# Attention of a two-layer diffusion step: the softmax division moved from the probabilities to the outputs

## The chip, the cores and the metric

The kernel runs on one core of a Trainium2 chip. The metric is the device time of one execution in microseconds (us), the median of three runs. One execution was also recorded by the hardware profiler, instruction by instruction; that record is the trace, and its summary is the profile's page.

## The reference, cut to what matters

One step of a hybrid backbone with two layers. Each layer is a half-step SwiGLU feed-forward block, a token mixer, and another half-step feed-forward block; the mixer of layer 0 is attention, that of layer 1 a spatial gating unit. Only the attention is touched here. It has 128 context tokens and 256 latent tokens, 16 heads of 64 numbers: 8 of neighbourhood attention (NA, with a bias on the latent scores) and 8 of grouped-query attention (GQA, no bias, 2 key heads).

```python
s = einsum(q * D ** -0.5, k)             # per head: 128 x 128 (context), 256 x 384 (latent)
p = softmax(s, axis=-1)                  # exp(s - max) / sum
o = einsum(p, v)                         # 64 numbers per query
```

Context queries see the 128 context keys of the step. Latent queries see 256 latent keys and 128 cached keys in one softmax. The outputs of all heads are concatenated and multiplied by `w_out`.

## The kernel before, in words

The program is written out by engine, each engine with its own list of instructions in a fixed order and waits on semaphores between them. Weights come in 1 MB panels (`raw`), which ScalarE rounds to a high part (`w_hi`, 1.9 us) and VectorE completes with a low part (`w_lo`); every weight product is three TensorE passes over high and low parts. The activations that feed a weight product are split in the same way, into `x_hi` and `x_lo`.

The attention stage stands between the panels of the q/k/v projection and those of the output projection (`Q_OUT0`, four panels). Heads go in eight pairs, in the order `TURNS = (0, 4, 1, 5, 2, 6, 3, 7)`: pairs under 4 are NA, the others GQA, so NA and GQA alternate, and turn n is the n-th pair. A turn has three steps, `s = 3n, 3n+1, 3n+2`: the context queries (below called C, 128 keys) and the two blocks of 128 latent queries (L1 and L2, 384 keys). All 128 queries of a step lie on the partitions, and both heads of the pair are handled together. A step goes through these stations:

- `scores(s)`, TensorE: two products into banks 5 and 6, or 0 and 1 in alternate steps. It waits for the exponentials of step s-2, which free the banks.
- `top(s)`, VectorE: for latent NA steps the bias is added, then the negated row maximum is taken (`nmax`).
- `softmax(s)`, ScalarE: exponential into `prob`, with the row sum in `rsum`.
- `normalise(s)`, VectorE: reciprocal of the sum, and a product over the whole of `prob` (128 x 768 numbers in a latent step).
- `p_transposes(s)`, TensorE: two or six transposes of 128 x 128 into banks 3 and 4, which are used in every step, so that they wait for the copy of step s-1.
- `put_pT(s)`, ScalarE: the copy of the transposed probabilities out of the banks (`pT_ctx`, `pT_lat`).
- `values(n)`, TensorE, once per turn: the products with v, transposed outputs (head numbers on the partitions, tokens along the row) into bank 7 or 2. It stands in step 3n+3, behind the transposes of that step.
- `o_hi(n)` on ScalarE and `o_lo(n)` on VectorE split the output straight from the bank into `x_hi` and `x_lo`.

TensorE runs two steps ahead: in step i it does `scores(i+2)`, then `p_transposes(i)`, and in every third step `values`. In steps 0 to 2 TensorE and ScalarE also finish the last transposes of q (`TR_LATE`, copied by `put_group`, semaphore `tr_act`). The last turn is folded into the first panel of the output projection (`last_pair`): TensorE does two output banks, the last transposes, two more banks, `values(7)`, and the other four banks. The split of the second output panel (`split(Q_OUT0 + 1)`) stands on ScalarE behind `o_hi(7)` and on VectorE behind `o_lo(7)`.

## Time and profile before

| what | value |
|---|---|
| median of 3 runs | 1561.32 us (1557.76 to 1566.09) |
| profiled execution, its time | 1559.92 us |
| its span in the trace | 1558.1 us |
| TensorE busy | 1519.7 us, 98% of the span |
| VectorE busy | 1073.2 us, 69% |
| ScalarE busy | 616.3 us, 40% |
| mean granted clock of TensorE | 0.995 of full speed |
| attention stage, first scores to the second output panel | 412.4 to 479.9 us |

The span is what the instructions cover; 1.8 us of the execution's time lie around it. TensorE's busy share is that of matmuls that overlap each other's fill and drain, so a high share doesn't say that the engine never waits. The attention stage is about 67 us, or 4% of the span.

### The profile page before, as it was taken

The numbers are of one execution on the slowest core, as the hardware profiler recorded it, in microseconds if no ns is written. First come the engines' busy times: TensorE is split into PE (matmuls) and PEld (weight loads), VectorE is DVE, ScalarE is ACT, GpSimd is POOL, SyncE is SP. The second block draws the span as 40 slices with busy tenths as digits, with TensorE's granted clock in tenths as the row PEclk, the third lists the DMA queues.
The fourth block names the chain that finished last, engine by engine and source line by source line (L and its number), as shares of the span: only waits on it lengthen the run. The fifth ranks groups of instructions, "written<-read, shape, count | busy, mean of one in ns | idle before, by whom it ended". The sixth has DMA issues, their size and how long they took to land.

```text
span 1558.1 us, 23355 instructions
## 1 busy us (share of the span) xinstructions
PE 1519.7 (98%) x9159; PEld 1491.8 (96%) x9159; DVE 1073.2 (69%) x1423; ACT 616.3 (40%) x840; POOL 74.0 (5%) x59
## 2 busy tenths in 40 slices
PE   6999999989899999999999999999999999999999
PEld 6899999989759999999999999999999999999999
DVE  6886777868897866768877667797767567443323
ACT  3452332164583643322355233226643246333221
POOL 2000000023100100000020000002000010000000
PEclk9999999989999999999999999999999999999999
DMA  9345465736403244465624545563552533333332
GB/s 386 112 141 211 166 228 205 261 139 230 139 1 140 104 172 178 180 250 193 241 86 154 220 162 216 216 252 130 195 206 82 216 109 108 135 111 133 135 112 91
DMA packets 49937, 262.68 MB, mean 169 GB/s; under 512 B 6608, under 2 KB 7888, under 8 KB 27984
## 3 DMA queue, kind: packets, MB, share of 16 engines
q1 hardware_dynamic: 49872, 261.79, 45.9%
q8 instruction: 44, 0.72, 0.2%
q14 instruction: 21, 0.17, 0.0%
HBM read 259.54 MB, written 2.23 MB: 168 GB/s over the span
## 4 chain that ended last, share of the span: by engine, by line
PE 84%; DVE 6%; issue 4%; DMA 2%; ACT 2%; SPq 1%; POOL 0%; DVEq 0%; ACTq 0%
PE ps L1288 24%; PE ps L1290 24%; PE ps L1289 24%; PE ps L1322 3%; PE ps L1325 3%; PE ps L1323 3%; DVE mprod L827 2%; ACT w_hi L537 1%; DMA raw<-panels 1%; DMA raw_x<-panels 1%; DVE x_lo L890 1%; DVE w_lo L819 1%; DVE h L1011 1%; PE ps L1612 1%; PE ps L1516 1%
## 5 line engine op out<-in xcount | busy, mean ns | idle before, releaser
L819 DVE TENSOR_TENSOR w_lo<-raw,w_hi 128x2048 fp32r<-128x2048 f32 x163 | 373.2, 2289 | 305.0 <-ACT w_hi L537 303.6
L537 ACT ACTIVATE w_hi<-raw 128x2048 fp32r<-128x2048 f32 x164 | 314.2, 1916 | 666.7 <-PE ps L1290 506.4
L1288 PE MATMUL ps<-x_hi,w_hi 128*128 128x384 f32 (+1 forms) x1520 | 515.9, 339 | 9.8 <-DVE x_lo L890 8.6
L1289 PE MATMUL ps<-x_lo,w_hi 128*128 128x384 f32 (+1 forms) x1520 | 513.1, 338 | 0.0
L1290 PE MATMUL ps<-x_hi,w_lo 128*128 128x384 f32 (+1 forms) x1520 | 512.7, 337 | 0.0
L827 DVE SCALAR_TENSOR_TENSOR mprod<-mraw,cB 128x1024 f32<-128x1024 f32 x256 | 313.2, 1224 | 7.8
L1288 PEld LDWEIGHTS ps<-x_hi,w_hi 128*128 128x128 f32 x1520 | 286.6, 189 | 13.2 <-issue 7.4
L1289 PEld LDWEIGHTS ps<-x_lo,w_hi 128*128 128x128 f32 x1520 | 286.9, 189 | 0.7
L1290 PEld LDWEIGHTS ps<-x_hi,w_lo 128*128 128x128 f32 x1520 | 286.6, 189 | 0.0
L1290 PE MATMUL ps<-act_hi,w_lo 128*128 (+1 forms) x832 | 279.6, 336 | 0.0
L1288 PE MATMUL ps<-act_hi,w_hi 128*128 (+1 forms) x832 | 279.6, 336 | 0.0
L1289 PE MATMUL ps<-act_lo,w_hi 128*128 (+1 forms) x832 | 279.6, 336 | 0.0
L1288 PEld LDWEIGHTS ps<-act_hi,w_hi 128*128 128x128 f32 x832 | 156.4, 188 | 0.0
L1289 PEld LDWEIGHTS ps<-act_lo,w_hi 128*128 128x128 f32 x832 | 156.4, 188 | 0.0
L1290 PEld LDWEIGHTS ps<-act_hi,w_lo 128*128 128x128 f32 x832 | 156.4, 188 | 0.0
L1322 PE MATMUL ps<-w_hi,x_hi 128*128 128x256 f32 x408 | 116.0, 284 | 3.0 <-ACT x_hi L564 2.4
L1323 PE MATMUL ps<-w_lo,x_hi 128*128 128x256 f32 x408 | 115.4, 283 | 0.0
L1325 PE MATMUL ps<-w_hi,x_lo 128*128 128x256 f32 x408 | 114.3, 283 | 0.0
L1322 PEld LDWEIGHTS ps<-w_hi,x_hi 128*128 128x128 f32 x408 | 77.7, 191 | 4.5 <-issue 4.5
L1323 PEld LDWEIGHTS ps<-w_lo,x_hi 128*128 128x128 f32 x408 | 77.8, 191 | 0.0
L1325 PEld LDWEIGHTS ps<-w_hi,x_lo 128*128 128x128 f32 x408 | 77.2, 191 | 0.0
L504 POOL TENSOR_TENSOR sqsum<-sq 128x384 f32<-128x384 f32 x6 | 9.7, 1621 | 1004.1 <-ACT sq L578 731.1
(154 smaller groups left out, 1148.4 us busy)
## 6 DMA issues: line engine op xcount, KB each, us to landing
raw<-panels SPq DMA_DIRECT2D x164, 1024.0 KB, 5.2
mraw<-mod_rows SPq DMA_DIRECT2D x128, 512.0 KB, 3.5
raw_x<-panels SPq DMA_DIRECT2D x5, 1024.0 KB, 6.0
mshift<-mod_rows SPq DMA_DIRECT2D x8, 512.0 KB, 15.5
mscale<-mod_scale SPq DMA_DIRECT2D x6, 512.0 KB, 12.2
bias<-na_bias SPq DMA_DIRECT2D x4, 512.0 KB, 6.4
h<-x_in_t SPq DMA_DIRECT2D x1, 1536.0 KB, 11.0
out<-h SPq DMA_DIRECT2D x4, 384.0 KB, 2.3
```

Source lines behind the costliest of these rows:

```text
L537: nc.scalar.activation(w_hi[q0 % 2][:, :], raw[q0 % 2][:, :], ACT.Copy).then_inc(hi_done, 1)
L819: nc.vector.tensor_tensor(w_lo[q0 % 2][:, :], raw[q0 % 2][:, :], w_hi[q0 % 2][:, :].bitcast(F32), ALU.subtract).then_inc(lo_done, 1)
L827: nc.vector.scalar_tensor_tensor(product[:, :], rows, 1.0, cB[:, cond, :], ALU.mult, ALU.mult, accum_out=out[:, cond:cond + 1]).then_inc(m ...
L890: last = nc.vector.scalar_tensor_tensor(x_lo[:, m, cols], h[:, m, cols], aT[:, m, cond:cond + 1], x_hi[:, m, cols].bitcast(F32), ALU.mult, ...
L1011: last = nc.vector.scalar_tensor_tensor(h[:, m, cols], ps[:, m, cols], gT[:, m, cond:cond + 1], h[:, m, cols], ALU.mult, ALU.add)
L1288: mm(out, w[0][:, cols], xs[0], start=start, stop=False)
L1289: mm(out, w[0][:, cols], xs[1], start=False, stop=False)
L1290: return mm(out, w[1][:, cols], xs[0], start=False, stop=stop)
L1322: mm(out, x_hi[:, k, tok], hi[:, cols], start=(k == 0), stop=False)
L1323: mm(out, x_hi[:, k, tok], lo[:, cols], start=False, stop=False)
L1325: last = mm(out, x_lo[:, k, tok], hi[:, cols], start=False, stop=(k == KD - 1))
L1516: last = nc.tensor.transpose(ps[:, 3 + a, P * k:P * k + P], prob[:, s % 3, a, P * k:P * k + P], ident[:, :])
```

## The change

The probabilities are no longer divided. The exponentials are transposed and multiplied with v as they are, and the outputs are divided by the sums. Since outputs lie with the tokens along the row, the reciprocals are needed along the row too. Per turn, `divisor` takes the six reciprocals of the turn (three steps, two heads) in one VectorE instruction, repeats each 64 times with a copy into `tmp[:, 2]` (128 x 384), TensorE transposes that in three pieces into bank 2 (`divisor_rows`), ScalarE copies the bank to `tmp[:, 1]` (`put_divisor`), and VectorE multiplies bank 7 with it into `tmp[:, 0]` (`o_divided`), from where `o_hi` and `o_lo` read. Bank 2 is no longer a second bank for the outputs. The copies out of the transposed probabilities' banks are shared: VectorE takes those of C steps in all turns, and of L1 steps in GQA turns; ScalarE keeps the rest.

```diff
--- before.py
+++ after.py
@@ -139,8 +139,8 @@
         hms = sb("hms", [P, 12])
         hrs = sb("hrs", [P, 12])
         nmax = sb("nmax", [P, 3, 2])
-        rsum = sb("rsum", [P, 3, 2])
-        rinv = sb("rinv", [P, 3, 2])
+        rsum = sb("rsum", [P, 2, 3, 2])
+        rinv = sb("rinv", [P, 4, 2])
         vss = sb("vss", [P, TT, KD])
 
 
...
@@ -340,6 +343,9 @@
         def span(s):
 
             return NCTX if s % 3 == 0 else T
+
+        def copied_by_vector(s):
+            return s % 3 == 0 or (s % 3 == 1 and TURNS[s // 3] >= 4)
 
         def scored(s):
 
...
@@ -699,41 +705,48 @@
                 act.wait_ge(nmax_done, s + 1)
                 if s >= 3:
                     act.wait_ge(pT_pe, s - 2)
+                if s >= 6 and s % 3 == 0:
+                    act.wait_ge(rinv_done, s // 3 - 1)
                 for a in range(2):
                     last = nc.scalar.activation(prob[:, s % 3, a, 0:span(s)], scored(s)[:, a, :], ACT.Exp,
-                                                bias=nmax[:, s % 3, a:a + 1], accum_out=rsum[:, s % 3, a:a + 1])
+                                                bias=nmax[:, s % 3, a:a + 1], accum_out=rsum[:, s // 3 % 2, s % 3, a:a + 1])
                 last.then_inc(exp_done, 1)
 
             def put_pT(s):
                 pair, kind = divmod(s, 3)
                 act.wait_ge(pT_pe, s + 1)
-                if kind == 0:
-                    if pair >= 2:
-                        act.wait_ge(o_pe, pair - 1)
-                    nc.scalar.activation(pT_ctx[:, pair % 2, :, :], ps[:, 3:5, 0:P], ACT.Copy).then_inc(pT_done, 1)
-                else:
-                    if pair:
-                        act.wait_ge(o_pe, pair)
-                    nc.scalar.activation(pT_lat[:, :, :, P * (kind - 1):P * kind],
-                                         ps[:, 3:5, 0:T].rearrange("p a (k q) -> p a k q", k=3), ACT.Copy) \
-                        .then_inc(pT_done, 1)
+                if pair:
+                    act.wait_ge(o_pe, pair)
+                nc.scalar.activation(pT_lat[:, :, :, P * (kind - 1):P * kind],
+                                     ps[:, 3:5, 0:T].rearrange("p a (k q) -> p a k q", k=3), ACT.Copy) \
+                    .then_inc(pT_done, 1)
+
+            def put_divisor(turn):
+                act.wait_ge(div_pe, turn + 1)
+                if turn:
+                    act.wait_ge(o_scaled, turn)
+                nc.scalar.activation(tmp[:, 1, 0:T], ps[:, DIV_BANK, 0:T], ACT.Copy).then_inc(div_done, 1)
 
             def o_hi(turn):
-                act.wait_ge(o_pe, turn + 1)
-                nc.scalar.activation(x_hi[:, TURNS[turn], 0:T], ps[:, O_BANK[turn % 2], 0:T], ACT.Copy).then_inc(oh_done, 1)
+                act.wait_ge(o_scaled, turn + 1)
+                nc.scalar.activation(x_hi[:, TURNS[turn], 0:T], tmp[:, 0, 0:T], ACT.Copy).then_inc(oh_done, 1)
 
             softmax(0)
             put_group(8)
             put_group(9)
             softmax(1)
             for i in range(STEPS):
-                put_pT(i)
+                if not copied_by_vector(i):
+                    put_pT(i)
+                if i and i % 3 == 0:
+                    put_divisor(i // 3 - 1)
                 if i + 2 < STEPS:
                     softmax(i + 2)
                 for j in TR_LATE.get(i, ()):
                     put_group(j)
-                if i and i % 3 == 0:
+                if i > 3 and i % 3 == 1:
                     o_hi(i // 3 - 1)
+            put_divisor(7)
             o_hi(7)
             split(Q_OUT0 + 1, 0)
             down(Q_OUT0, KD // 2, lambda: split_spare(1))
...
@@ -1169,30 +1182,55 @@
                     link(nc.vector.tensor_tensor(v, v, bias[:, kind - 1, 2 * pair:2 * pair + 2, :], ALU.add))
                 nc.vector.tensor_reduce(nmax[:, s % 3, :], scored(s), AX.X, ALU.max, negate=True).then_inc(nmax_done, 1)
 
-            def normalise(s):
-                dve.wait_ge(exp_done, s + 1)
-                link(nc.vector.reciprocal(rinv[:, s % 3, :], rsum[:, s % 3, :]))
-                v = prob[:, s % 3, :, 0:span(s)]
-                nc.vector.tensor_tensor(v, v, rinv[:, s % 3, :, None].to_broadcast([P, 2, span(s)]), ALU.mult) \
-                    .then_inc(prob_done, 1)
+            def put_pT(s):
+                pair, kind = divmod(s, 3)
+                dve.wait_ge(pT_pe, s + 1)
+                if kind == 0:
+                    if pair >= 2:
+                        dve.wait_ge(o_pe, pair - 1)
+                    nc.vector.tensor_copy(pT_ctx[:, pair % 2, :, :], ps[:, 3:5, 0:P]).then_inc(pT_done, 1)
+                else:
+                    dve.wait_ge(o_pe, pair)
+                    nc.vector.tensor_copy(pT_lat[:, :, :, P * (kind - 1):P * kind],
+                                          ps[:, 3:5, 0:T].rearrange("p a (k q) -> p a k q", k=3)).then_inc(pT_done, 1)
+
+            def divisor(turn):
+                dve.wait_ge(exp_done, 3 * turn + 3)
+                if turn:
+                    dve.wait_ge(div_pe, turn)
+                link(nc.vector.reciprocal(rinv[:, 0:TT, :], rsum[:, turn % 2, :, :]))
+                nc.vector.tensor_copy(tmp[:, 2, 0:T].rearrange("p (t a d) -> p t a d", a=2, d=HD),
+                                      rinv[:, 0:TT, :, None].to_broadcast([P, TT, 2, HD])).then_inc(rinv_done, 1)
+
+            def o_divided(turn):
+                dve.wait_ge(o_pe, turn + 1)
+                if turn:
+                    dve.wait_ge(ol_done, turn)
+                dve.wait_ge(div_done, turn + 1)
+                nc.vector.tensor_tensor(tmp[:, 0, 0:T], ps[:, O_BANK, 0:T], tmp[:, 1, 0:T], ALU.mult) \
+                    .then_inc(o_scaled, 1)
 
             def o_lo(turn):
-                pair = TURNS[turn]
+                dve.wait_ge(o_scaled, turn + 1)
                 dve.wait_ge(oh_done, turn + 1)
-                nc.vector.tensor_tensor(x_lo[:, pair, 0:T], ps[:, O_BANK[turn % 2], 0:T], x_hi[:, pair, 0:T].bitcast(F32),
+                nc.vector.tensor_tensor(x_lo[:, TURNS[turn], 0:T], tmp[:, 0, 0:T], x_hi[:, TURNS[turn], 0:T].bitcast(F32),
                                         ALU.subtract).then_inc(ol_done, 1)
 
             dve.wait_ge(bias_in, 64)
             top(0)
             top(1)
-            normalise(0)
             for i in range(STEPS):
                 if i + 2 < STEPS:
                     top(i + 2)
-                if i + 1 < STEPS:
-                    normalise(i + 1)
-                if i > 3 and i % 3 == 1:
-                    o_lo(i // 3 - 1)
+                if copied_by_vector(i):
+                    put_pT(i)
+                if i and i % 3 == 0:
+                    o_divided(i // 3 - 1)
+                if i % 3 == 2:
+                    divisor(i // 3)
+                    if i > 3:
+                        o_lo(i // 3 - 1)
+            o_divided(7)
             o_lo(7)
             split(Q_OUT0 + 1, 0)
             down(Q_OUT0, KD // 2, 1, (0, 1), 1.0, MOD_M + MOD_IN, MOD_OUT, spare=1)
...
@@ -1508,7 +1546,7 @@
                 last.then_inc(s_pe, 1)
 
             def p_transposes(s):
-                pe.wait_ge(prob_done, s + 1)
+                pe.wait_ge(exp_done, s + 1)
                 if s:
                     pe.wait_ge(pT_done, s)
                 for a in range(2):
...
@@ -1516,12 +1554,20 @@
                         last = nc.tensor.transpose(ps[:, 3 + a, P * k:P * k + P], prob[:, s % 3, a, P * k:P * k + P], ident[:, :])
                 last.then_inc(pT_pe, 1)
 
+            def divisor_rows(turn):
+                pe.wait_ge(rinv_done, turn + 1)
+                if turn:
+                    pe.wait_ge(div_done, turn)
+                for t in range(TT):
+                    last = nc.tensor.transpose(ps[:, DIV_BANK, P * t:P * t + P], tmp[:, 2, P * t:P * t + P], ident[:, :])
+                last.then_inc(div_pe, 1)
+
             def values(turn):
 
                 pair = TURNS[turn]
+                if turn:
+                    pe.wait_ge(o_scaled, turn)
                 pe.wait_ge(pT_done, 3 * turn + 3)
-                if turn >= 2:
-                    pe.wait_ge(ol_done, turn - 1)
                 v, cache = (v_na, vc_na) if pair < 4 else (vg_, vc_g)
                 for keys, out_cols, start, stop in ((-1, slice(0, P), True, True), (0, slice(P, T), True, False),
                                                     (1, slice(P, T), False, False), (2, slice(P, T), False, True)):
...
@@ -1529,7 +1575,7 @@
                         cols = slice(HD * (2 * pair + a), HD * (2 * pair + a) + HD) if pair < 4 else slice(HD * a, HD * a + HD)
                         w = cache[:, cols] if keys == 2 else v[:, keys + 1, cols]
                         moving = pT_ctx[:, turn % 2, a, :] if keys < 0 else pT_lat[:, a, keys, :]
-                        last = mm(ps[HD * a:HD * a + HD, O_BANK[turn % 2], out_cols], w, moving, start=start, stop=stop)
+                        last = mm(ps[HD * a:HD * a + HD, O_BANK, out_cols], w, moving, start=start, stop=stop)
                 last.then_inc(o_pe, 1)
 
             pe.wait_ge(tr_act, 5)
...
@@ -1548,24 +1594,27 @@
                     pe.wait_ge(tr_act, 10)
                 if i + 2 < STEPS:
                     scores(i + 2)
+                if i == 3:
+                    pe.wait_ge(tr_act, 13)
+                if i and i % 3 == 0:
+                    divisor_rows(i // 3 - 1)
                 p_transposes(i)
                 for j in TR_LATE.get(i, ()):
                     pe.wait_ge(tr_act, j - 1)
                     transposed(j)
-                if i == 3:
-                    pe.wait_ge(tr_act, 13)
                 if i and i % 3 == 0:
                     values(i // 3 - 1)
 
             def ready_attn(m):
                 if m == 5:
                     pe.wait_ge(exp_done, STEPS - 1)
+                    pe.wait_ge(ol_done, 6)
                 elif m == 0:
                     pe.wait_ge(exp_done, STEPS)
                 elif m == 4:
                     pe.wait_ge(pT_done, STEPS)
                 elif m == 7:
-                    pe.wait_ge(ol_done, 7)
+                    pe.wait_ge(o_scaled, 8)
                 elif m == 2:
                     pe.wait_ge(ol_done, 8)
 
...
@@ -1574,6 +1623,7 @@
                 some((5, 6))
                 p_transposes(STEPS - 1)
                 some((0, 1))
+                divisor_rows(NH - 1)
                 values(NH - 1)
                 return some((4, 3, 7, 2))
 
```

What stands in each engine's list is read from the two programs. First VectorE, from the maximum of turn 2's C step (an NA turn) to the work behind the maximum of its L2 step; `nmax<-ps` are the maxima, `ps<-ps,bias` the bias. Before:

```order
L1170 TENSOR_REDUCE nmax<-ps 128x2
L1174 RECIPROCAL rinv<-rsum 128x2
L1176 TENSOR_TENSOR prob<-prob,rinv 128x768
L1182 TENSOR_TENSOR x_lo<-ps,x_hi 128x384
L1169 TENSOR_TENSOR ps<-ps,bias 128x2x256
L1170 TENSOR_REDUCE nmax<-ps 128x2
L1174 RECIPROCAL rinv<-rsum 128x2
L1176 TENSOR_TENSOR prob<-prob,rinv 128x2x128
L1169 TENSOR_TENSOR ps<-ps,bias 128x2x256
L1170 TENSOR_REDUCE nmax<-ps 128x2
L1174 RECIPROCAL rinv<-rsum 128x2
L1176 TENSOR_TENSOR prob<-prob,rinv 128x768
```

And of the change, for the same stretch:

```order
L1183 TENSOR_REDUCE nmax<-ps 128x2
L1194 COPY pT_lat<-ps 128x6x128
L1182 TENSOR_TENSOR ps<-ps,bias 128x2x256
L1183 TENSOR_REDUCE nmax<-ps 128x2
L1201 RECIPROCAL rinv<-rsum 128x6
L1202 COPY tmp<-rinv 128x384
L1216 TENSOR_TENSOR x_lo<-tmp,x_hi 128x384
L1182 TENSOR_TENSOR ps<-ps,bias 128x2x256
L1183 TENSOR_REDUCE nmax<-ps 128x2
L1191 COPY pT_ctx<-ps 128x256
L1210 TENSOR_TENSOR tmp<-ps,tmp 128x384
```

The three products over `prob` (turn 1's L2 step, turn 2's C and L1) and the three small reciprocals are gone. In their place are the copy of turn 1's L1 step (`pT_lat<-ps`), the reciprocal and the repeat of turn 1 (`rinv<-rsum` of six, `tmp<-rinv`) behind turn 2's L1 maximum, the copy of turn 2's C step, and the product with the divisors.

Next TensorE, at the end of turn 1: the scores of its L2 step (GQA), the transposes of turn 1's C step, and the values of turn 0. Before:

```order
L1507 MATMUL ps<-kT_g,qT_g 128x384 x2
L1516 MATMUL ps<-ident,prob 128x128 x2
L1532 MATMUL ps<-pT_ctx,v_na 64x128 x2
L1532 MATMUL ps<-pT_lat,v_na 64x256 x4
L1532 MATMUL ps<-pT_lat,vc_na 64x256 x2
```

And of the change:

```order
L1545 MATMUL ps<-kT_g,qT_g 128x384 x2
L1562 MATMUL ps<-ident,tmp 128x128 x3
L1554 MATMUL ps<-ident,prob 128x128 x2
L1578 MATMUL ps<-pT_ctx,v_na 64x128 x2
L1578 MATMUL ps<-pT_lat,v_na 64x256 x4
L1578 MATMUL ps<-pT_lat,vc_na 64x256 x2
```

Three transposes of `tmp` (the repeated reciprocals of turn 0) stand between the scores and the transposes of the probabilities, seven times in the loop; an eighth group stands in front of the last `values`.

Last ScalarE, at the end of the stage. Before:

```order
L703 ACTIVATE prob,rsum<-ps,nmax 128x384 x2
L723 ACTIVATE x_hi<-ps 128x384
L717 ACTIVATE pT_lat<-ps 128x6x128 x2
L723 ACTIVATE x_hi<-ps 128x384
L537 ACTIVATE w_hi<-raw 128x2048 x3
```

And of the change:

```order
L711 ACTIVATE prob,rsum<-ps,nmax 128x384 x2
L732 ACTIVATE x_hi<-tmp 128x384
L720 ACTIVATE pT_lat<-ps 128x6x128
L728 ACTIVATE tmp<-ps 128x384
L732 ACTIVATE x_hi<-tmp 128x384
L543 ACTIVATE w_hi<-raw 128x2048 x3
```

The last high part (`x_hi`) is now read from `tmp` and so stands behind VectorE's product, which is not in this list; the copy of the divisors (`tmp<-ps`) is new, one per turn.

## Rows read from the trace of the kernel before

Rows of the timeline give the start in us, the duration, the engine, line, operation, output and inputs; in brackets the idle time before it and what ended it.

**Rows 1.** The page: span, and busy time of each engine.

```profile
span 1558.1 us, 23355 instructions
PE 1519.7 (98%) x9159; PEld 1491.8 (96%) x9159; DVE 1073.2 (69%) x1423; ACT 616.3 (40%) x840; POOL 74.0 (5%) x59
```

**Rows 2.** Windows, from one pair's last scores group to the next pair's.

```profile
core 0: us, PE busy (x) PEld busy (x) DVE busy (x) ACT busy (x) POOL busy (x), PEclk, DMA share, GB/s
424.57:431.45 6.88, 5.87 (x44) 3.37 (x43) 4.81 (x9) 5.50 (x17) 0.00 (x0) 1.00 0.01 2
451.42:457.55 6.13, 5.84 (x43) 3.37 (x42) 5.16 (x11) 5.22 (x16) 0.00 (x0) 1.00 0.00 0
457.55:464.48 6.93, 5.94 (x43) 3.37 (x43) 6.76 (x13) 5.44 (x16) 0.00 (x0) 1.00 0.00 0
```

**Rows 3.** Windows of 2 us where the granted clock changes.

```profile
418.00:420.00 2.00, 0.61 (x5) 0.45 (x6) 1.97 (x4) 1.38 (x6) 0.00 (x0) 1.00 1.00 371
420.00:422.00 2.00, 2.00 (x11) 1.67 (x13) 1.19 (x3) 1.23 (x4) 0.00 (x0) 0.56 0.96 262
```

**Rows 4.** Timeline, TensorE: one group of turn 1, then turns 5 and 6.

```profile
421.71 1.65 PE L1507 MATMUL ps<-kT_g,qT_g 64*128 64x384 f32 x4
...
451.42 0.92 PE L1507 MATMUL ps<-kT_g,qT_g 64*128 64x384 f32 x4
...
452.48 0.41 PE L1516 MATMUL ps<-ident,prob 128*128 128x128 f32 x2
...
454.49 0.49 PE L1507 MATMUL ps<-kT_na,qT_na 64*128 64x128 f32 x4
...
454.91 0.88 PE L1516 MATMUL ps<-ident,prob 128*128 128x128 f32 x6
...
455.71 0.92 PE L1507 MATMUL ps<-kT_na,qT_na 64*128 64x384 f32 x4
...
456.75 0.64 PEld L1516 LDWEIGHTS ps<-ident,prob 128*128 128x128 f32 x6 [0.73 <-DVE prob L1176]
...
457.55 0.92 PE L1507 MATMUL ps<-kT_na,qT_na 64*128 64x384 f32 x4
...
459.17 0.44 PE L1516 MATMUL ps<-ident,prob 128*128 128x128 f32 x2 [0.70 <-DVE prob L1176]
```

**Rows 5.** Timeline, VectorE and ScalarE, in the same stretch.

```profile
452.39 0.96 DVE L1170 TENSOR_REDUCE nmax<-ps 128x2 f32<-128x768 f32 x1 [0.35 <-PE ps L1507]
...
455.82 0.81 ACT L717 ACTIVATE pT_lat<-ps 128x768 f32<-128x768 f32 x1 [0.58 <-PE ps L1516]
...
458.50 0.15 DVE L1174 RECIPROCAL rinv<-rsum 128x2 f32<-128x2 f32 x1
...
459.03 0.69 DVE L1169 TENSOR_TENSOR ps<-ps,bias 128x512 f32<-128x512 f32 x1
...
460.75 0.58 ACT L703 ACTIVATE prob<-ps,nmax 128x384 f32<-128x384 f32 x1 [0.63 <-DVE nmax L1170]
```

**Rows 6.** Groups by line and form, whole kernel, VectorE.

```profile
L1176 DVE TENSOR_TENSOR prob<-prob,rinv 128x768 f32<-128x768 f32 x16 | 15.3, 958 | 0.6
L1182 DVE TENSOR_TENSOR x_lo<-ps,x_hi 128x384 fp32r<-128x384 f32 x8 | 4.4, 552 | 6.2 <-ACT x_hi L723 6.2
L884 DVE COPY sqsum<-ps 128x384 f32<-128x384 f32 x5 | 2.8, 557 | 15.3 <-PE ps L1375 15.3
L1248 DVE TENSOR_SCALAR wsn<-wsT,rs 128x1024 f32<-128x1024 f32 x3 | 2.1, 750 | 1.0 <-POOL rs L522 1.0
```

**Rows 7.** Timeline: the first values group (turn 0) and the end of the stage.

```profile
426.72 0.44 PE L1532 MATMUL ps<-pT_ctx,v_na 128*64 128x128 f32 x4 [0.86 <-ACT qT_g L668]
...
473.47 0.44 PE L1532 MATMUL ps<-pT_ctx,vg_ 128*64 128x128 f32 x4
...
475.25 0.49 ACT L723 ACTIVATE x_hi<-ps 128x384 fp32r<-128x384 f32 x1 [2.98 <-PE ps L1532]
...
479.92 0.45 PE L1288 MATMUL ps<-x_hi,w_hi 128*128 128x384 f32 x1 [0.27 <-DVE w_lo L819]
```

More of the change, by code:

```diff
@@ L262, in build @@
         exp_done = sem("exp_done")
-        prob_done = sem("prob_done")
+        rinv_done = sem("rinv_done")
+        o_scaled = sem("o_scaled")
+        div_pe = sem("div_pe")
+        div_done = sem("div_done")
         pT_pe = sem("pT_pe")
@@ L692, in _ @@
                 if g == 7:
-                    nc.scalar.activation(rsum[:, 2, 0:1], mhalf[:, 0:1], ACT.Exp)
+                    nc.scalar.activation(rsum[:, 0, 2, 0:1], mhalf[:, 0:1], ACT.Exp)
                 for i in TR_AFTER[g]:
@@ L1652 @@
 S_BANK = (5, 0)
-O_BANK = (7, 2)
+O_BANK, DIV_BANK = 7, 2
 TR_AFTER = ((), (), (), (), (0, 1), (2, 3), (4, 5), (6, 7), ())
@@ L1663, in tr_bank @@
 def tr_bank(i):
-    return 3 + i % 2 if i < 8 else O_BANK[i % 2]
+    return 3 + i % 2 if i < 8 else (O_BANK, DIV_BANK)[i % 2]
 _OUTS = [(P, KD, T), (1, 1, NCTX, NH, HD), (1, 1, NCTX, NH, HD), (1, 1, NCTX, 2, HD), (1, 1, NCTX, 2, HD)]
```

## The prediction

> **What bounds the kernel now.** I read the page first: 1519.7 us of TensorE in a span of 1558.1 [rows 1], so outside the attention any gain on another engine is covered by weight products. Then the windows, cut at TensorE's last scores group of each turn (S2; S0, S1 and S2 are a turn's three scores groups, T0, T1, T2 its transposes, V the values, D the new transposes of the reciprocals). An interval from a GQA turn's S2 to an NA turn's takes 6.13 us, one from NA to GQA 6.93 [rows 2]. In the longer VectorE is busy for 6.76 of 6.93 us; in the shorter for 5.16 of 6.13. TensorE's 5.84 and 5.94 us look nearly full too, but pipelined matmuls overstate it, so I read the timeline for spacings [rows 4]. S0 takes 0.42 until the next group can start (454.49 to 454.91) though it is busy for 0.49; a 384-column group, busy for 0.92, then takes 0.85. Six transposes take 0.80 (454.91 to 455.71). T0 and V together take 2.01 (452.48 to 454.49). One interval therefore needs of TensorE S2 0.85, T0 and V 2.01, S0 0.42, T1 0.80, S1 0.85, T2 0.80: 5.73 us. The rest is waiting: 0.21 in front of T0 and 0.19 in front of T2 when the next turn is NA (5.73 + 0.40 = 6.13), and 1.2 when VectorE has the bias in front of it, where the chain of waits runs through VectorE and T0 starts at 459.17 instead of 458.40 [rows 4]. So VectorE's queue bounds half of the intervals, and TensorE is only 0.4 us from bounding the others.
>
> **The change, part by part.**
>
> VectorE loses, per turn, two products of 0.96 [rows 6], one of 256 numbers, 0.42 (on the line through 0.552 for 384 and 0.958 for 768), and three reciprocals; it gains a reciprocal of 0.15 [rows 5], the repeat, a division of 128 x 384 from PSUM, which I price as the existing subtraction of that form, 0.55 [rows 6], a C copy of 256 numbers, 0.42 by the same line, and in GQA turns a copy of 128 x 768 out of PSUM. That copy has no row; a copy of 384 takes 0.557 against 0.552 for a two-operand instruction of that width, so 768 will take what the product of 768 takes, 0.96 [rows 6]. For the repeat, SBUF to SBUF with 384 numbers out, the bounds are 0.28 (750 ns for 1024 numbers of a one-operand instruction, in proportion) and 0.557 (a copy of the same width from PSUM) [rows 6]. I take 0.557: same operation, same width. Balance: 2.8 us off and about 1.7 (NA) or 2.6 (GQA) on. VectorE stops being full.
>
> The Trainium skill ("VectorE: DVE Perf Modes", Mode 2×_2P) says that an fp32 copy runs at two numbers a cycle if source and destination lie in SBUF, and not out of PSUM. The first half would give the repeat about 0.28 and the sum 0.8 less; the second agrees with the row of 0.557 for a PSUM copy.
>
> TensorE gains D, three transposes: half of six, 0.40, eight times, 3.2 us, all on the engine that is nearly full. The interval's own work becomes 6.13. That is the floor: the average now is 6.53, so the most that the loop can win is 0.4 per turn.
>
> Waits that stay or come. (a) T0 waited for the product; it now needs only the exponential and stands behind D, so 0.21 goes. (b) T2 waits for the copy of T1 out of the same banks: T1 to T2 is 1.84 where work takes 1.65, hence 0.19. It stays in NA turns. In GQA turns the copy is VectorE's, 0.96 instead of 0.81 [rows 5], so 0.34. (c) D waits for the reciprocals, and those stand on VectorE behind the next turn's L1 maximum. Count from S2 of a GQA turn at 0, next turn NA: D to 1.25, T0 and V to 3.26, S0 to 3.68, T1 to 4.48, S1 from 4.48, T2 from 5.67 (b), next S2 at 6.47, D could start at 7.32. VectorE: scores reach it 0.97 after their start (451.42 to 452.39 [rows 4, 5]), so 5.45; its copy of T1 ends at 5.5; bias and maximum run until 1.72 later (459.03 to 460.75 [rows 5]), less 0.1 that the next instruction overlaps, so 7.1; reciprocal with its self-wait 0.2; repeat 0.56; signal 0.12: 7.97. D waits 0.65 and with it T0, V and all behind. With the next turn GQA the maximum has no bias: the repeat ends about 0.75 earlier, no wait. Behind the repeat VectorE still has `o_lo`, then the L2 bias and maximum; those end at 9.9 or 3.4 after S2, and their exponential is wanted by S1 at about 5.1: covered by V. ScalarE gains a copy of 384 (0.49, as its existing one [rows 7]) and loses the C copy in all turns and one of 0.81 in GQA turns; it stays below 5.5 us an interval and is covered.
>
> So an interval from GQA to NA takes 6.13 + 0.34 = 6.47 (now 6.13), one from NA to GQA 6.13 + 0.19 + 0.65 = 6.97 (now 6.93). From turn 2's S2 to turn 7's there are three of the longer and two of the shorter: 33.85 against 33.05, **+0.8 us**. The interval before, now 6.88 [rows 2], is different: V of turn 0 waits until 426.72 for ScalarE's last copy of q [rows 7]. That wait moves ahead of D. ScalarE has one copy less before it and the exponentials come a product earlier; counting its list the copy ends about 1.3 us sooner, of which D and T0 take 0.4 and 0.35 back: **-0.4 us**, with bounds of -1.4 (all kept) and +0.2.
>
> End of the stage. From turn 7's S2 to T2 of the loop, D adds 0.40 and the 0.4 of waits for products go: 0. Then D stands ahead of the last V, 0.40. After it, V starts at 473.47, ScalarE's high part at 475.25, then the split of the second panel, for which TensorE waits until 479.92 [rows 7]. The wait is already there, so everything put into that chain counts: the division 0.55 and a handover of 0.03. Together **+1.0 us**. If TensorE had had other work it would cost nothing; it has none.
>
> Sum: 0.8 - 0.4 + 0 + 1.0 = +1.4 us on 1559.92, the profiled execution's own time: 1561.3. The shown median is 1.4 us above that execution, so I name 1561.5 and let the range take the spread.
>
> **The rivals.**
>
> (1) *Forecast: given back.* VectorE's relief turns into D on TensorE and the wait (c), with a longer end: 1561.3. Chance 0.60.
>
> (2) *The relief is kept.* Waits (b) and (c) vanish if VectorE runs its list sooner than I count (repeat at 0.28, small instructions overlapping). All intervals at 6.13: 30.65, -2.4; start down to -1.4; end +1.0: 1557.1. For it: (c) is a difference of two sums over eight instructions. Against: (b) is two row spacings. Chance 0.26.
>
> (3) *VectorE's queue delays D in every turn,* as it would if the copies out of PSUM are dearer than 0.96: every interval 6.13 + 0.34 + 0.65 = 7.12, five give 35.6, +2.55; start +0.2, end +1.0: 1563.7. It decides, meaning over 0.5%, only when an interval reaches 7.6 us or more, 1.1 above the present mean in each of some seven. Chance 0.08.
>
> (4) *Slower: TensorE's clock falls for the stage.* The granted clock fell to 0.56 in 420 to 422, right after two microseconds in which TensorE was busy for 0.61 of 2.00 [rows 3]: between its levels, 1.2 and 2.4 GHz. A scores group then took 1.65 instead of 0.92 [rows 4], 1.8 times. An interval at the lower level would be 6.13 x 1.8 = 11.0, 4.5 more, over some seven and a half: +34 us, 1594. Against it: in all intervals of rows 2 the clock stayed at 1.00, with 1.94 of each 5.73 us in transposes, and the change leaves TensorE fewer gaps. It decides if the engine's work per interval thins out as in the window from 418. Chance 0.04.
>
> On this the Trainium skill ("TensorE: Matmul & The Clock Gate", Part 4: PE-mode transpose) says that a transpose does not count as activity for the full clock as a matmul does. That speaks against more transposes; the trace shows full clock throughout a stage with 14 transposes per turn, and 17 will hardly differ.
>
> (5) *A gain over 0.5%.* It would need 7.8 us of a stage whose floor allows 2.4 in the loop. Chance 0.02.
>
> **Numbers.** 0.5% (7.8 us) is about what a measurement of this kernel can tell from no change. Cases 1 to 3 lie within 4 us of the time before; with the spread of single runs (3.6 below and 4.8 above the median) they give "same" 0.92, slower 0.05, faster 0.03. The range takes 1557.1 and 1563.7 and, for the median's own wandering, another 1 to 3 us: 1556 to 1567.
>
> **What the profile would show.** Right: VectorE clearly below 6.76 us in NA-to-GQA intervals; these intervals at about 7.0, with TensorE idle in front of L1562 until the repeat (L1202), and about 6.5 the other way; the second output panel 7.0 us behind the start of the last V (now 6.45). Wrong: D never waits (then case 2), the repeat at half its price, T0 waiting for VectorE's copies, or a clock under 1.00 behind 424. Most likely to be wrong is (c): a shift of 0.3 us in VectorE's list changes three intervals by as much.

## Result, and the profile after

The changed kernel takes 1570.9 us (median of 10 runs, 1566.2 to 1572.76), the one before 1562.28 (10 runs, 1557.76 to 1566.72). The ratio is 1.0053 [1.0043, 1.0064]: 8.6 us slower, outside the range of 1556 to 1567. The profiled execution took 1570.92 us.

The page of the changed kernel, span and engines, against [rows 1]:

```profile
span 1569.1 us, 23425 instructions
PE 1531.6 (98%) x9183; PEld 1505.1 (96%) x9183; DVE 1067.1 (68%) x1411; ACT 614.4 (39%) x836; POOL 74.1 (5%) x59
```

VectorE is busy for 6.1 us less. TensorE is busy for 11.9 us more, and has only 24 matmuls more. Eight groups of three small transposes, 3.2 us of work, can't be 11.9. So I cut the execution into three pieces at starts of `w_lo` panels (VectorE's low parts, numbered from 0 to 162): up to panel 40, in front of the attention; 40 to 43, the attention stage; 43 to 162, all that follows.

| us | to panel 40 | 40 to 43 | 43 to 162 |
|---|---|---|---|
| before | 412.41 | 78.27 | 1049.34 |
| changed | 417.71 | 77.41 | 1055.79 |

The stage that the diff rewrites is 0.86 us shorter. The loss lies outside it, 6.45 us behind it and 5.3 ahead of it. (The piece ahead wanders, 412.4 to 417.7 over the 13 profiles of this study. Part of it doesn't: from the first to the last product of 384 columns, the first feed-forward block takes 224.58 us before and 228.68 in the changed kernel, 4.1 more. What wanders is the stretch between this block and the attention, 92.4 to 96.2 us, with no order by layout. What follows therefore rests on the last piece and on medians.)

Where behind it? The start of a low part at the head and at the end of ten panels of the second feed-forward block, VectorE's timeline of the kernel before:

```profile
636.20 2.29 DVE L819 TENSOR_TENSOR w_lo<-raw,w_hi 128x2048 fp32r<-128x2048 f32 x1 [3.98 <-ACT w_hi L537]
...
719.40 2.29 DVE L819 TENSOR_TENSOR w_lo<-raw,w_hi 128x2048 fp32r<-128x2048 f32 x1 [0.73 <-ACT w_hi L537]
```

and of the changed kernel:

```profile
641.20 2.29 DVE L832 TENSOR_TENSOR w_lo<-raw,w_hi 128x2048 fp32r<-128x2048 f32 x1 [5.21 <-ACT w_hi L543]
...
725.04 2.29 DVE L832 TENSOR_TENSOR w_lo<-raw,w_hi 128x2048 fp32r<-128x2048 f32 x1 [0.80 <-ACT w_hi L543]
```

Ten panels take 83.20 us before and 83.84 now. VectorE isn't the cause: it sits idle ahead of these instructions for longer than before. A panel is 48 TensorE products with 384 columns, so they follow each other every 173.3 ns before and every 174.7 ns now. A window of 100 us in the last feed-forward block shows the same thing without VectorE. Kernel before, then changed (columns as in [rows 2]):

```profile
1400.00:1500.00 100.00, 100.00 (x579) 100.00 (x578) 35.84 (x22) 28.73 (x20) 0.00 (x0) 1.00 0.36 126
```

```profile
1400.00:1500.00 100.00, 100.00 (x575) 100.00 (x574) 36.58 (x22) 29.55 (x22) 0.00 (x0) 1.00 0.36 126
```

TensorE is never idle in either, the granted clock is 1.00 in both, the DMA moves the same bytes, and it gets through 575 matmuls instead of 579. The spacing is uniform (between 1400 and 1460 us no two starts lie further apart than 0.18 us), with no gap at a panel's head. So no wait was added: every such product is 0.8% slower, in code that the diff doesn't touch.

In two stretches of the changed kernel the loss per product is larger: in the first feed-forward block and in the gating unit's output projection the products follow each other every 176.5 to 176.7 ns, where the kernel before has 173.3 to 173.5. A window of 60 us in that projection, kernel before and then changed:

```profile
1211.00:1271.00 60.00, 60.00 (x348) 60.00 (x347) 31.09 (x34) 18.34 (x13) 0.00 (x0) 1.00 0.48 176
```

```profile
1215.00:1275.00 60.00, 60.00 (x342) 60.00 (x341) 30.12 (x30) 16.65 (x10) 0.00 (x0) 1.00 0.49 177
```

The stretches account for the last piece: three feed-forward blocks of 1,296 such products take 1.72 us more each (224.47 to 226.19), and the projection's 384 products 1.28 more (66.39 to 67.67), together 6.44 of the 6.45 us.

What the diff does reach is where buffers lie. Buffers are placed one behind the other in slots of 32 bytes per partition. `rsum` grew from 24 to 48 bytes, one slot to two (`rinv`'s 24 to 32 still fit in one). So `x_hi`, `x_lo`, `x2_hi`, `x2_lo`, `act_hi`, `act_lo` and all else behind `rsum` moved by 32 bytes. The weights (`raw`, `w_hi`, `w_lo`), which lie ahead of it, did not. The addresses below follow from the programs' lists of buffers; no trace shows them.

| byte address per partition | `w_hi` | `x_hi` | `act_hi` |
|---|---|---|---|
| before | 45184 (0 mod 64) | 112032 (32 mod 64) | 161312 (32 mod 64) |
| changed | 45184 (0) | 112064 (0) | 161344 (0) |

`x2_hi` and `x2_lo` hold the activations of the later gate and up panels (the views print them as `x_hi` and `x_lo`, without the number); they stand at the same place modulo 64 as `x_hi` in every kernel here. Their tiles and those of `act_hi` lie a multiple of 64 bytes apart. The tiles of `x_hi` itself are 386 numbers long and lie 1544 bytes apart, so each stands 8 bytes further on modulo 64, and the 386-column products that read them hardly differ: 178.8 ns before, 179.0 in the changed kernel. The theory below is therefore about the 384-column products with `x2` and `act`.

**The stage itself.** The windows of two intervals, against [rows 2]:

```profile
435.29:441.94 6.65, 6.19 (x46) 3.69 (x46) 5.27 (x10) 5.28 (x16) 0.00 (x0) 1.00 0.01 2
441.94:448.36 6.42, 6.12 (x46) 3.69 (x45) 4.95 (x11) 4.77 (x16) 0.00 (x0) 1.00 0.00 1
```

From GQA to NA an interval takes 6.42 (was 6.13), from NA to GQA 6.65 (was 6.93). Turn 2's S2 to turn 7's is 32.78 us (was 33.03). The timeline around D, TensorE and VectorE, against [rows 4, 5]:

```profile
434.52 0.85 PE L1554 MATMUL ps<-ident,prob 128*128 128x128 f32 x6 [0.30 <-DVE pT_lat L1194]
435.29 0.92 PE L1545 MATMUL ps<-kT_na,qT_na 64*128 64x384 f32 x4
435.89 0.18 DVE L1201 RECIPROCAL rinv<-rsum 128x6 f32<-128x6 f32 x1
436.10 0.36 DVE L1202 COPY tmp<-rinv 128x384 f32<-128x384 f32 x1
436.52 0.55 PE L1562 MATMUL ps<-ident,tmp 128*128 128x128 f32 x3 [0.31 <-DVE tmp L1202]
```

Both forecast waits are here. T2 waits for VectorE's copy, and D starts at 436.52 where the spacing of a scores group (0.85) would have let it start at 436.14: 0.38 us. The end of the stage, VectorE, ScalarE and TensorE, against [rows 7]:

```profile
477.27 0.44 PE L1578 MATMUL ps<-pT_ctx,vg_ 128*64 128x128 f32 x4
479.05 0.56 DVE L1210 TENSOR_TENSOR tmp<-ps,tmp 128x384 f32<-128x384 f32 x1 [4.94 <-PE ps L1578]
479.64 0.53 ACT L732 ACTIVATE x_hi<-tmp 128x384 fp32r<-128x384 f32 x1 [1.77 <-DVE tmp L1210]
482.01 2.29 DVE L832 TENSOR_TENSOR w_lo<-raw,w_hi 128x2048 fp32r<-128x2048 f32 x1 [1.18 <-ACT w_hi L543]
484.36 0.44 PE L1326 MATMUL ps<-x_hi,w_hi 128*128 128x384 f32 x1 [0.97 <-DVE w_lo L832]
```

The second output panel starts 7.09 us behind the last V (forecast 7.0).

### The profile page after: what moved, and what is told of

It is laid out like the page before. It is cut to its first block, busy times and chain, and to the rows that moved or that the text cites. A ratio compares the mean times of both kernels' runs of the same rounds, so it can differ in the third digit from the quotient of the medians.

```text
span 1569.1 us, 23425 instructions
## 1 busy us (share of the span) xinstructions
PE 1531.6 (98%) x9183; PEld 1505.1 (96%) x9183; DVE 1067.1 (68%) x1411; ACT 614.4 (39%) x836; POOL 74.1 (5%) x59
## 4 chain that ended last, share of the span: by engine, by line
PE 86%; DVE 5%; issue 3%; DMA 3%; ACT 2%; SPq 1%; POOL 0%; DVEq 0%; ACTq 0%
PE ps L1326 25%; PE ps L1328 25%; PE ps L1327 25%; PE ps L1360 3%; PE ps L1361 3%; PE ps L1363 3%; DVE mprod L840 2%; DMA raw<-panels 1%; ACT w_hi L543 1%; DMA raw_x<-panels 1%; PE ps L1578 1%; DVE x_lo L903 1%; DVE w_lo L832 1%; DVE h L1024 1%; PE ps L1662 1%
```

## The experiments

The theory: where the buffers lie sets the pace of TensorE's 384-column products, and that is the whole loss (A); in the form that e5 and e6 test, it is how the two operands' addresses stand to each other modulo 64 bytes (R). Its rivals: the longer instruction lists of the changed program (B); the stage's new work and what it sets off later (C); or the place of one operand decides, whatever the other does (M for the moving operand, the activations; W for the weights). "Before" in the ratios is the kernel before, run on the same chip.

**e1: only the address.** The kernel before, with a slot added ahead of `x_hi`:

```diff
         vss = sb("vss", [P, TT, KD])
+        sb("pad", [P, 8])
```

> The kernel before with nothing changed but 32 bytes per partition allocated ahead of x_hi, so that x_hi, x_lo, x2, act_hi, act_lo and all that is allocated behind them stand 32 bytes higher, as they do in the changed kernel (its rsum and rinv are larger). No instruction is added. Theory A (place in memory: the 384-column products over these buffers are paced at 174.7 ns instead of 173.3, in the first FFN 176.7): 9 to 12 us slower than before, 1571 to 1574, with panels of 8.385 us in the last FFN instead of 8.318. Theory B (code: the longer instruction lists of the changed kernel put loops and instruction fetch elsewhere): no change, 1562. Theory C (the attention stage with its new waits): no change, 1562.

**e2: only the rest.** The changed kernel, with `rinv` placed behind `act_lo`, which gives the slot back:

```diff
-        rinv = sb("rinv", [P, 4, 2])
...
         act_lo = sb("act_lo", [P, KF, T], F32R)
+        rinv = sb("rinv", [P, 4, 2])
```

> The changed kernel with rinv allocated behind act_lo, so that x_hi and everything behind it stand at the addresses of before; same instructions as the changed kernel. Theory A: the attention stage's own effect is left, which the two traces put at -0.9 us up to the output projection: 1560 to 1563, panels of 8.318 us. Theory B: as the changed kernel, 1571. Theory C: 1571.

**e3: a slot of 64 bytes.** As e1, with `[P, 16]`.

> The kernel before with 64 bytes ahead of x_hi instead of 32. Theory A1 (what counts is the address modulo 64): as before, 1562. Theory A2 (a larger modulus, or any shift costs): slower, 1566 to 1574. Theories B and C: 1562.

Measured: e1 1569.37 us, ratio 1.0048 [1.0035, 1.0061]; e2 1562.38, 1.0003 [0.9991, 1.0016]; e3 1559.81, 0.9995 [0.9982, 1.0007]. An unused slot in the old kernel brings nearly the whole loss, and the new attention at the old addresses, with all its longer lists, brings none. e1 stayed under the 1571 to 1574 that were expected: in its profile the first feed-forward block ran at 174.7 ns, not at the changed kernel's 176.6. From panel 43 on e1 takes 1055.86 us (the changed kernel 1055.79), e2 1049.39 and e3 1049.21 (before 1049.34). So neither the new work nor the code is the cause. The move counts modulo 64: by 64 bytes nothing happens.

**e4: only the activations of the down projections.** The slot stands behind `region_d`, so `act_hi` and `act_lo` move and `x_hi` stays.

```diff
         sb("region_d", [P, KS, T])
+        sb("pad", [P, 8])
```

> The kernel before with 32 bytes between region_d and the buffers that share the memory of act_hi and act_lo: only the FFN activations (moving operand of the down panels), the attention buffers and the gating unit's move, x_hi, x_lo and x2 stay. Theory A: only the down panels slow down, 832 x 3 products of 384 columns by 1.4 ns each = +3.5 us (to +8 if it is 3.4 ns as in the first FFN), 1565 to 1570, gate and up panels unchanged at 8.32. Theories B and C: 1562.

Measured 1563.49, ratio 1.0012 [1.0002, 1.0021]: the range was missed, the direction not. By TensorE's own starts in the last three blocks: the products with `x2_hi` and `x2_lo`, which stayed, follow each other every 173.3 ns, as before; those with `act_hi` and `act_lo`, which moved, every 174.7 (before 173.3). So the pace follows each buffer by itself. Of the 3.5 us that were expected (832 x 3 = 2,496 products at 1.4 ns) the profile has 2.5 from panel 43 on and 0.7 in the first block. The medians have 2.3, and the interval reaches from 0.3 to 3.3.

**e5: everything moves together.** A slot ahead of `h`, so weights and activations both stand 32 bytes further on.

```diff
+        sb("pad", [P, 8])
         h = sb("h", [P, KD, T])
```

> The kernel before with 32 bytes ahead of h, its first buffer: the weights' buffers w_hi and w_lo move to 32 modulo 64 (from 0) and x_hi, x_lo, x2, act_hi and act_lo to 0 modulo 64 (from 32). Theory M (the address of the moving operand alone counts, 32 modulo 64 is the faster): as the 32-byte pad before, gate and up panels of the second FFN at 8.384 us and a median of 1569. Theory R (it counts that weights and moving operand stand at different places modulo 64): panels of 8.320 us and 1561.

**e6: the weights move to where the activations are.** As e5, with `rinv` behind `act_lo`, so that `x_hi` keeps 112032 and `w_hi` goes to 45216: both 32 mod 64.

> The kernel before with 32 bytes ahead of h and rinv allocated behind act_lo, so that only the buffers from h to rsum move by 32 bytes, the weights' buffers among them (now 32 modulo 64), and x_hi, x_lo, x2, act_hi, act_lo stay where they are (32 modulo 64). Theory M: panels of 8.320 us, 1561. Theory R: weights and moving operand now stand at the same place modulo 64, so 8.384 us and 1569. Theory W (the weights' own address counts): slower or faster here and in the run with everything moved alike.

Measured: e5 1562.45, ratio 1.0000 [0.9989, 1.0012]; e6 1575.9, 1.0088 [1.0073, 1.0103]. e5 has the activations at 0 mod 64, as the slow kernels have, and is as fast as before; e6 has them at the fast kernels' own address and is the slowest of all. So the activations' place alone doesn't decide. Nor does the weights': they stand at 32 in both. Only the relation is left. (Nor can it be e6's other move, `rinv` to the end: e2 has it and is fast.) Here is the window of 1400 to 1500 us of e5, then of e6:

```profile
1400.00:1500.00 100.00, 100.00 (x579) 100.00 (x578) 35.17 (x21) 28.73 (x20) 0.00 (x0) 1.00 0.36 126
```

```profile
1400.00:1500.00 100.00, 100.00 (x571) 100.00 (x570) 36.26 (x22) 29.05 (x22) 0.00 (x0) 1.00 0.35 126
```

579 as before, and 571. The theory has e6's sign and not its size: I had expected about 1569. The ten panels of e6, first and last start in VectorE's timeline:

```profile
631.05 2.29 DVE L820 TENSOR_TENSOR w_lo<-raw,w_hi 128x2048 fp32r<-128x2048 f32 x1
...
715.32 2.29 DVE L820 TENSOR_TENSOR w_lo<-raw,w_hi 128x2048 fp32r<-128x2048 f32 x1 [0.77 <-ACT w_hi L538]
```

84.27 us for 480 products, 175.6 ns each. (The first gap falls one panel ahead of the rows shown above for the other kernels, in the same block.)

**e11: the changed kernel with the weights moved instead.** e2 plus e5's slot: `w_hi` at 32, `x_hi` at 0 mod 64, as the changed kernel has it.

> The changed kernel with rinv behind act_lo and 32 bytes ahead of h: weights' buffers at 32 modulo 64, x_hi, x_lo, x2, act_hi, act_lo at 0 modulo 64, as these last are in the changed kernel as it was given. Theory R (slow only where weights and moving operand stand at the same place modulo 64): panels of 8.320 us in the second FFN and 1562, as with rinv moved alone. Theory M (the moving operand's own place): 8.384 us and 1570.

Measured 1562.63, ratio 0.9991 [0.9979, 1.0004], and 1049.38 us from panel 43 on. The changed kernel is cured with its activations left where they are, by moving the weights. All layouts together, the pace in the second to fourth feed-forward blocks:

| weights / `x2` and `act`, mod 64 | kernels | 43 to 162, us | per product, ns |
|---|---|---|---|
| 0 / 32 | before, e2, e3, e7, e8, e9, e10 | 1049.21 to 1049.44 | 173.3 |
| 32 / 0 | e5, e11 | 1049.36, 1049.38 | 173.3 |
| 0 / 0 | changed, e1 | 1055.79, 1055.86 | 174.7 |
| 32 / 32 | e6 | 1058.11 | 175.6 |

(e4 has both: 0 / 32 for `x2`, 0 / 0 for `act`.) In the 0 / 0 kernels the gating unit's output projection runs at 176.7 ns, as shown above, and in e4, where it is 0 / 0 too, at 174.7. What makes the difference between the two is not shown.

**e7: the reciprocals ahead of the maximum.** With the layout out of the way, the stage's own steps can be tried. e2 with `divisor` moved in VectorE's list:

```diff
             for i in range(STEPS):
+                if i % 3 == 2:
+                    divisor(i // 3)
                 if i + 2 < STEPS:
                     top(i + 2)
```

> The changed kernel at the addresses of before (rinv behind act_lo), with the reciprocals and their repeat taken ahead of the next turn's L1 maximum on VectorE instead of behind it. If the wait of TensorE's divisor transposes for the repeat (0.38 us in front of each in the NA-to-GQA intervals) is a cost of its own: those intervals go from 6.65 to about 6.27 us and the loop from turn 2 to turn 7 from 32.78 to 31.6, together -1.2 to -1.5 us against the same kernel without this. If the delay is only handed on (the bias, the maximum and the exponential come 0.54 us later and the scores of the next turn wait for them): no change.

**e8: and the second panel's split earlier.** e7 with `split(Q_OUT0 + 1, 0)` ahead of `put_divisor(7)` on ScalarE and of `o_divided(7)` on VectorE.

> The same, and the split of the second output panel placed ahead of the last outputs on both engines (ahead of the divisors' copy on ScalarE and of the division on VectorE), where both stood idle for 3 to 6 us. If the chain division, high part, split, low part is what delays the second output panel (the end of the stage is 0.84 us longer than before in the trace), that panel starts right behind the first: -0.9 to -1.4 us more, 1559 to 1560, faster than before by 0.1% or a little more. If the end is bound elsewhere (banks 7 and 2 free later): no change against the version without it.

**e9: all copies back on ScalarE.** e2 with `copied_by_vector` returning False.

> The changed kernel at the addresses of before with all copies of the transposed probabilities back on ScalarE (the sharing undone, the division still on the outputs). The wait of the L2 transposes in GQA turns falls from 0.34 to 0.19 us if ScalarE is free when the L1 transposes are done, the loop from turn 2 to turn 7 from 32.78 to some 32.4; if ScalarE's list (exponential of L2, copy of L1, exponential of the next C step) becomes the bound, the next L2 scores wait for that exponential and the loop grows by 0.3 to 1 us. In both cases 1561 to 1563, a ratio of 1.000 within 0.001: the sharing is worth less than a measurement of this kernel tells.

**e10: the early split alone, in the kernel before.** The split stands ahead of `o_hi(7)` and `o_lo(7)`.

> The kernel before with only the split of the second output panel placed ahead of the last outputs' high and low parts. If the end of the stage is bound by that split, the 0.27 to 0.6 us that TensorE waited for it go and the second panel starts that much sooner: 15.44 us from turn 7's L2 scores becomes 15.0 to 15.1, 1560.9 (ratio 0.9997, not to be told from 1 in the time, but in the trace).

| | loop, turn 2 to 7 | 40 to 43 | median | ratio to before |
|---|---|---|---|---|
| e2 | 32.78 | 77.41 | 1562.38 | 1.0003 [0.9991, 1.0016] |
| e7 | 31.82 | 76.46 | 1559.52 | 0.9987 [0.9976, 0.9999] |
| e8 | 31.82 | 75.28 | 1560.41 | 0.9990 [0.9981, 0.9999] |
| e9 | 32.92 | 77.41 | 1561.72 | 0.9993 [0.9981, 1.0004] |
| e10 | 33.04 | 76.13 | 1563.06 | 0.9999 [0.9987, 1.0011] |

e7's timeline: the repeat ends 1.2 us ahead of the scores, and D follows them at their own spacing, 0.85.

```profile
434.96 0.36 DVE L1202 COPY tmp<-rinv 128x384 f32<-128x384 f32 x1
436.52 0.92 PE L1545 MATMUL ps<-kT_g,qT_g 64*128 64x384 f32 x4
437.37 0.55 PE L1562 MATMUL ps<-ident,tmp 128*128 128x128 f32 x3
```

The NA-to-GQA interval is 6.32 us, which is my floor of 6.13 plus the 0.19 of T2's wait; the loop gained 0.96 us, where 1.2 was expected. So the wait was a cost of its own. (The medians of e2 and e7 lie 2.9 us apart; the trace explains no more than 0.95 of that.) In e8 the low part is ready before the products need it, and TensorE's stop of 0.97 us in front of the second panel is gone:

```profile
472.66 1.91 ACT L543 ACTIVATE w_hi<-raw 128x2048 fp32r<-128x2048 f32 x1
474.29 0.44 PE L1578 MATMUL ps<-pT_ctx,vg_ 128*64 128x128 f32 x4
474.60 2.29 DVE L832 TENSOR_TENSOR w_lo<-raw,w_hi 128x2048 fp32r<-128x2048 f32 x1 [3.50 <-ACT w_hi L543]
476.81 0.55 DVE L1210 TENSOR_TENSOR tmp<-ps,tmp 128x384 f32<-128x384 f32 x1
```

That is 1.18 us in the trace. In the medians e8 can't be told from e7, nor e10 from before, where the trace shows 0.54 us (76.67 at full clock to 76.13): such steps lie below what the runs tell apart. e9 costs 0.14 us in the loop, neither the gain of 0.4 nor the loss of 0.3 to 1 that were expected: sharing the copies between the engines is worth nearly nothing. The interval from GQA to NA gets shorter, 6.27 (T2 waits for ScalarE's 0.81 and not VectorE's 0.96), the one from NA to GQA longer, 6.79, with D's wait grown:

```profile
447.36 0.55 PE L1567 MATMUL ps<-ident,tmp 128*128 128x128 f32 x3 [0.45 <-DVE tmp L1207]
```

e7 and e8 are some 10 us faster than the changed kernel. Against the one before they are 0.1% faster, which is at the edge of the interval, so a gain over it is not shown.

## Why the prediction was wrong

**The step that failed** is in the first paragraph: "outside the attention any gain on another engine is covered by weight products". From this it follows that the sum had terms for the stage alone and none for the other 96% of the span. True of other engines' work, it says nothing of TensorE's own pace. The two lines of the diff that resize `rsum` and `rinv` were costed at nothing, without a word on what lies behind them. The missing term is 1.33 ns times 5,568 products of 384 columns with `x2` or `act` (four blocks of 1,296, and 384 in the gating unit's output projection), 7.4 us at the least. The stretches that ran at 176.6 ns add to it: 8.1 us in e1's profile (1.6 in the first block, 6.5 from panel 43 on) and 10.5 in the changed kernel's (4.1 and 6.45). The medians show 8.6 between the kernels. None of the five rivals had it, so "slower" stood at 0.05. The page's sentence that the engine is 98% busy was the warning: where one engine fills the span, half a per cent of its pace weighs more than the whole stage could give.

**The mechanism in the stage** was the forecast one, with these sizes:

| term | forecast | measured |
|---|---|---|
| D's wait, NA to GQA | 0.65 | 0.38 |
| interval NA to GQA | 6.97 | 6.65 |
| interval GQA to NA | 6.47 | 6.42 |
| loop, turn 2 to 7 | +0.8 | -0.25 |
| first scores to turn 2's S2 | -0.4 | +0.1, at full clock |
| end of the stage | +1.0 | +0.84 |
| sum, stage | +1.4 | +0.74, at full clock |

The first term carries the loop. D started 7.65 us after the GQA turn's S2, where I had 7.97: 0.20 of the 0.32 is the repeat, priced at 0.557 and measured at 0.36. It is the groups view of VectorE in 417 to 490 us that shows this, and the prices that were right:

```profile
L1210 DVE TENSOR_TENSOR tmp<-ps,tmp 128x384 f32<-128x384 f32 x8 | 4.5, 558 | 9.8 <-PE ps L1578 9.4
L1194 DVE COPY pT_lat<-ps 128x768 f32<-128x768 f32 x4 | 3.8, 958 | 1.2 <-PE ps L1554 1.2
L1202 DVE COPY tmp<-rinv 128x384 f32<-128x384 f32 x8 | 2.9, 360 | 0.3
```

The division took 558 ns (priced 0.55) and the copy of 768 numbers out of PSUM 958 (priced 0.96). The bounds given for the repeat, 0.28 and 0.557, hold the measured 0.36; I had chosen the wrong end, by the width of the row and not by its source. The Trainium skill ("VectorE: DVE Perf Modes", Mode 2×_2P) puts an fp32 copy within SBUF at two numbers a cycle, and this row is much nearer to that than to the PSUM copy's.

The start of the stage was mis-sized too. I had the last copy of q end 1.3 us sooner. It starts 11.3 to 11.4 us behind the first scores with the new attention, and 12.1 with the old at full clock, so 0.7 sooner, and the 0.75 of D and T0 take all of it back. (With 1.3 the terms of that sentence give -0.55, and not the -0.4 that stands there.) The handover of 0.12 us from VectorE to TensorE in the count of D is 0.06 in the rows above.

What the profile before shows at the start has one more part, which isn't a matter of waits. [rows 3] show the granted clock at 0.56 in 420 to 422. The same 20 us of the kernel before and, below, of e1, whose attention is word for word the same:

```profile
412.00:432.00 20.00, 15.93 (x100) 9.55 (x98) 15.36 (x26) 13.54 (x41) 0.00 (x0) 0.91 0.42 138
```

```profile
412.00:432.00 20.00, 16.03 (x111) 9.99 (x109) 16.90 (x27) 13.89 (x41) 0.00 (x0) 1.00 0.42 138
```

The fall comes in four of seven profiles of the old attention (before, e3, e4, e6; the stage is then 78.17 to 78.30 us) and not in the others (e1, e5: 76.65 and 76.68; e10, with its earlier split, 76.13). With the new attention it came in none of six. It costs 1.6 us. So at full clock the change costs the stage 0.74 us (77.41 against 76.67), and the 0.86 us that it seemed to gain are this fall's absence. Whether the change prevents it or six profiles missed it stays open. Nor do the two microseconds ahead of it decide: TensorE was busy for 0.61 of 2.00 there [rows 3], but in e5 for 0.72 of 2.00 in 418 to 420, and the clock stayed at 1.00. Rival 4, a lower clock for the whole stage, did not come: with 17 transposes per turn the rows show 1.00, and the doubt that the Trainium skill ("TensorE: Matmul & The Clock Gate", Part 4: PE-mode transpose) raises about transposes was not borne out at this mix.

**Against the rivals.** Case 1, the relief given back, is what the stage shows, less sharply. Case 2, the relief kept, was nearer in the loop than in my sum (-0.25 between -2.4 and +0.8), and e7 shows what part of it was to be had: D's wait goes with one reordering, T2's does not. Case 3 failed at its price, since VectorE's copy costs what I took.

## What to carry to other kernels

Where one engine is busy for nearly the whole span, read a diff for what it does to that engine everywhere: a buffer that grows by one slot moves all that is placed behind it, and here 32 bytes cost more than ten times what the rewritten stage did (8.6 us against 0.74). Compare the pace in stretches that the change doesn't touch before explaining anything in those it does; when it differs, put the old addresses back (one line) and time that first. When operands of long runs of products come from two buffers, try both offsets: it costs one unused slot.

## What the runs showed of the hardware

- TensorE's products of 384 columns with both operands rounded (fp32r) ran every 173.3 ns when the stationary and the moving operand stood at different places modulo 64 bytes (0 and 32), every 174.7 ns, in some stretches 176.7, when both stood at 0, and every 175.6 ns when both stood at 32. That the two meet in reading SBUF is a guess, for which only the uniform spacing speaks; why 32/32 costs more per product than 0/0 is open.
- Products of 386 columns, whose moving operand's tiles stand at eight different places modulo 64, ran every 178.8 ns before, 179.0 in the changed kernel and 178.0 in e6.
- The products in which weights are the moving operand, 256 columns, hardly care: a q/k/v panel takes 8.90 us before and 8.94 to 8.95 in the changed kernel, e1 and e6. But in e3, which has the layout of before modulo 64, it takes 8.96, so modulo 64 isn't the whole of it there.
- In the changed kernel's first feed-forward block the spacing was 176.6 ns, in e1's, with the same layout, 174.7. One execution each; not explained.
- The time up to the attention differs by up to 5.3 us between executions (412.4 to 417.7), where single runs of one kernel spread over 4 to 9 us.
